# Layer 0 of a two-block transformer kernel: latent norms, up-projections and rotary rotation in one stage, with f32r products in 128-row chunks

## What is computed

```python
p = h @ w_in                                   # 384 cq | 256 ckv | 32 kr | 512 gq | 128 gk | 128 gv
qa = (rmsnorm(cq, q_norm) @ w_q_up)            # 8 heads of 64 + 32
kva = (rmsnorm(ckv, kv_norm) @ w_kv_up)        # 8 heads of 64 (keys) + 64 (values)
q_rope, k_rope = apply_rope(q_rope, ra), apply_rope(kr, ra)    # latent tokens only
qa = concat([q_nope, q_rope]) * (96 ** -0.5)
ka = concat([k_nope, broadcast(k_rope)])
qb, kb = apply_rope(rmsnorm(gq per head), rb) * (64 ** -0.5), apply_rope(rmsnorm(gk per head), rb)
```

## Time and profile before

| | |
|---|---|
| median of 3 runs | 3511.75 us (3507.56 to 3515.62) |
| profiled execution | 3518.39 us; its span 3516.5 us, mean granted TensorE clock 0.931 |
| PE busy | 3104.1 us, 88% of the span |
| DVE, ACT, POOL busy | 1457.6, 761.2, 237.0 us |
| ab_in, first to last PE instruction | 53.1 to 156.4 us |
| norm_qk, ab_up and rope together | 157.0 to 299.3 us |
| PE / DVE / ACT busy from 157.0 to 299.3 | 128.9 / 57.7 / 21.2 us |

### The profile page before, as it was taken

How to read it: one execution, slowest core, us unless ns; L and a number is a source line. 1 busy time by engine, 2 the same in 40 slices (tenths; PEclk the granted TensorE clock), 3 DMA queues, 4 the chain that set the end, 5 groups by cost and what they waited for, 6 DMA issues and landing times. The chain is left out here.

```text
span 3516.5 us, 48978 instructions
## 1 busy us (share of the span) xinstructions
PE 3104.1 (88%) x19193; PEld 2127.7 (61%) x19193; DVE 1457.6 (41%) x2568; ACT 761.2 (22%) x1482; POOL 237.0 (7%) x435
## 2 busy tenths in 40 slices
PE   7999998799886599977987759989999999899998
PEld 5734667333333598753333337867888788678886
DVE  4316564300000533852000026455555683655555
ACT  3114571211111302821111111142110111221101
POOL 0000040111111200001111110000000000000000
PEclk9999999899998699988998769999999999999998
DMA  7376812999998422349999973113334164123421
GB/s 259 123 269 153 207 18 95 384 419 419 419 419 349 132 72 61 74 164 388 419 419 418 419 283 115 60 49 90 95 107 109 39 104 61 49 72 95 125 72 54
DMA packets 352386, 675.09 MB, mean 192 GB/s; under 512 B 68643, under 2 KB 277636, under 8 KB 296775
## 3 DMA queue, kind: packets, MB, share of 16 engines
q1 hardware_dynamic: 336460, 635.42, 52.0%
q0 software_dynamic: 13664, 31.49, 2.5%
q10 hardware_dynamic: 2067, 5.48, 0.4%
HBM read 642.80 MB, written 45.09 MB: 196 GB/s over the span
## 5 line engine op out<-in xcount | busy, mean ns | idle before, releaser
L3838 ACT ACTIVATE ffn_mixed<-ffn_mixed 128x512 f32<-128x512 f32 x44 | 27.8, 632 | 393.8 <-DVE ffn_mixed L3759 393.8
L2054 DVE TENSOR_TENSOR moe0b_hidden<-moe0b_hidden,moe0b_wide_ps 64x512 f32<-64x512 f32 (+1 forms) x21 | 12.7, 602 | 229.1 <-ACT moe0b_hidden L2051 229.1
L2039 PE MATMUL moe0b_wide_ps<-moe_raw,moe0b_feats 128*64 128x512 f32 x208 | 95.7, 610 | 9.5 <-DMA moe_raw<-in_moe_w_up 9.5
L2054 DVE TENSOR_TENSOR moe1b_hidden<-moe1b_hidden,moe1b_wide_ps 64x512 f32<-64x512 f32 (+1 forms) x18 | 10.3, 573 | 224.1 <-ACT moe1b_hidden L2051 224.1
L2054 DVE TENSOR_TENSOR moe0b_second<-moe0b_second,moe0b_wide_ps 64x512 f32<-64x512 f32 (+1 forms) x20 | 12.2, 611 | 208.1 <-ACT moe0b_second L2051 208.1
L2054 DVE TENSOR_TENSOR moe1b_second<-moe1b_second,moe1b_wide_ps 64x512 f32<-64x512 f32 (+1 forms) x18 | 10.3, 572 | 211.4 <-ACT moe1b_second L2051 211.4
L2040 PE MATMUL moe0b_wide_ps<-moe_raw,moe0b_feats 128*64 128x512 f32 x208 | 95.9, 612 | 0.0
L3756 DVE TENSOR_SCALAR ffn_mixed<-ffn_gate_ps,all_cols 128x512 f32<-128x512 f32 x44 | 35.6, 810 | 145.3 <-PE ffn_up_ps L3688 141.1
L1496 DVE TENSOR_REDUCE attn_top<-attn_scores 128x1 f32<-128x768 f32 (+1 forms) x96 | 72.3, 776 | 37.1 <-PE attn_scores L1409 37.0
L1465 ACT ACTIVATE attn_probs_t<-attn_turned 128x512 f32<-128x512 f32 x112 | 63.4, 604 | 78.9 <-PE attn_turned L1423 78.9
L243 POOL CAST second_first_hi<-all_ahead 128x1024 fp32r<-128x1024 f32 x8 | 9.8, 1223 | 982.6 <-DMA all_ahead<-in_ffn_w_up 696.7
(11 more groups left out here) (998 smaller groups left out, 8681.3 us busy)
## 6 DMA issues: line engine op xcount, KB each, us to landing
moe_raw<-in_moe_w_gate SPq DMA_DIRECT2D x88, 1024.0 KB, 27.3
moe_raw<-in_moe_w_up SPq DMA_DIRECT2D x88, 1024.0 KB, 27.9
moe_raw<-in_moe_w_down SPq DMA_DIRECT2D x86, 1024.0 KB, 28.4
all_ahead<-in_ffn_w_up SPq DMA_DIRECT2D x88, 512.0 KB, 5.1
all_h<-in_moe_w_gate SPq DMA_DIRECT2D x26, 1024.0 KB, 26.8
all_h<-in_w_ada SPq DMA_DIRECT2D x23, 1024.0 KB, 5.5
all_h<-in_moe_w_down SPq DMA_DIRECT2D x21, 1024.0 KB, 28.3
ffn_down<-in_ffn_w_down SPq DMA_DIRECT2D x40, 512.0 KB, 3.6
```

The source lines that it names most:

```text
L2039: nc.tensor.matmul(wide_ps[n][LOW, :], x[:, c, :], gate[:, at], start=c == 0, stop=c == DC - 1)
L2054: return nc.vector.tensor_tensor(hidden[n][HIGH, 0:cols], hidden[n][HIGH, 0:cols], wide_ps[n][HIGH, 0:cols], ALU.mult)
L3838: nc.scalar.activation(mixed[s][:], mixed[s][:], ACT.Silu).then_inc(silu_ready, 1)
```

## The change

The three stages norm_qk, ab_up and rope become one, `up_stage`. In it:

- Queries and keys are computed in chunks of 128 rows instead of heads. The weights of the queries are loaded so that the rotary rows of four heads make a chunk (`q0`, `q1`) and the other rows of two heads make one (`q2` to `q5`). Two halves of 384 tokens take the place of 256 and 512. Every product is three f32r matmuls.
- The queries' products start from the raw latent times its gain; the root is applied to the result, when DVE takes it out of PSUM. The keys' and values' latent is scaled first.
- POOL gets work: the split of the query weights (beside ab_in), five of the ten squares, the rest part of the key and value weights, and the eight cosine products.
- The rotation has eight items: the shared key, the two rotary query chunks, four gq, gk.
- PSUM holds two slots of two banks, used in turn by 29 named uses (`UP_USES`); a use waits until the use before it in its slot has been taken.
- Units 16 to 23 of the conditioning move into ab_in, whose ring now has two slots (units 11 to 23); units 24 to 47 have a ring of three. ab_in starts with six DMAs of the query weights instead of units 11 and 12.
- The rotary tables are loaded over the query latent, so their five DMAs wait for `q5`.

```diff
-            own = [sb(f"ada_slot{n}", [PART, ada.GROUP])[:] for n in range(2)]
...
-            ada.place("in", own + [P.h[:].rearrange("p c n -> p (c n)")[:, n * ada.GROUP:(n + 1) * ada.GROUP] for n in range(3)], units)
-            early, late = units[0:2], units[2:]
+            units = range(FIRST_UNITS, 3 * DC)
+            ada.place("in", ada_slots[0:2], units)
+            coming_slots = [P.ahead[:].rearrange("p c n -> p (c n)")[:, n * ada.GROUP:(n + 1) * ada.GROUP] for n in range(2)]
+            ada.place("later", coming_slots + ada_slots[0:1], range(3 * DC, ada.GROUPS * DC))
...
-            at_unit = {8: early[0:1], 10: early[1:], 18: late[0:1], 19: late[1:2], 20: late[2:]}
+            at_unit = {11: (11,), 12: (12,), 13: (13,), 14: (14, 15), 15: (16,), 16: (17, 18), 17: (19,), 18: (20, 21), 19: (22,), 20: (23,)}
...
+        up_stage(nc, P, A, K, ada, weights, cq, ckv, lows, kr, gq, gk, qa, ka, va, distances)
```

The heart of `up_stage`, SP's tables and PE's products and first uses:

```diff
+            sp.wait_ge(ready, slots.made["q5"])
+            for q in range(QUADS):
+                sp.dma_start(rope_q[q * QUAD:(q + 1) * QUAD], K["rope_a"][rope_rows]).then_inc(tables_in, 16)
+            sp.dma_start(rope_g, K["rope_b"]).then_inc(tables_in, 16)
+            for u in range(33, 43):
+                ada.fetch(sp, u)
...
+            def q_rows(name, c, j):
+                cols = slice(j * PART, (j + 1) * PART)
+                for k, (w, x) in enumerate(((wq.hi, cq_hi), (wq.hi, cq_lo), (wq.lo, cq_hi))):
+                    for h in range(2):
+                        last = T.matmul(slot[slots.at[name]][:, h, 0:HALF], w[:, c, cols], x[:, c, h * HALF:(h + 1) * HALF],
+                                        start=c == 0 and k == 0, stop=c == QC - 1 and k == 2)
...
+            ada.multiply(pe, 24)
+            pe.wait_ge(cq_split, 1)
+            q_rows("q0", 0, 0)
...
+            spread("cq", NORM_CQ, 0)
+            q_product(1)
...
+            q_product(5)
+            ada.multiply(pe, 31)
...
+            k_product(0)
+            ada.multiply(pe, 32)
+            pe.wait_ge(tables_in, 16 * (2 + QUADS))
+            turn(0)
+            ada.multiply(pe, 33)
...
+            V.tensor_tensor(squares[0], cq[:, 0, :], cq[:, 0, :], ALU.mult).then_inc(squared_by["dve"], 1)
...
+            low_q(0)
...
+            emptied(dve, "cq")
+            take_rope(0)
```

More of the change, by code:

```diff
@@ L1235, in add_deep @@
     return take
-def load(slot, source, ring=0, after=None):
-    return Load(slot, source, ring, after)
-def product(operands, shape, take, load=0, engine=None, finish=None):
-    return Product(operands, shape, take, load, engine, finish)
 def wide(t):
@@ new lines, in v_product @@
+            def v_product(i):
+                enter(f"v{i}")
+                for n in range(2):
+                    rows = slice((2 * i + n) * PART, (2 * i + n + 1) * PART)
+                    for c in range(KVC):
+                        for k, (x, w) in enumerate(((ckv_hi, wkv_hi), (ckv_lo, wkv_hi), (ckv_hi, wkv_lo))):
+                            last = T.matmul(slot[slots.at[f"v{i}"]][:, n, :], x[:, c, rows], w[:, c, H_A * NOPE_A:],
+                                            start=c == 0 and k == 0, stop=c == KVC - 1 and k == 2)
+                last.then_inc(ready, 1)
@@ new lines, in spread, with turn @@
+            def spread(name, kind, group):
+                pe.wait_ge(inverted, group + 1)
+                enter(name)
+                quads.spread(slot[slots.at[name]], pick[:, kind], root[:, group, :], ready)
+            def turn(n):
+                x, rows = turn_rows[n]
+                enter(f"turn{n}")
+                T.matmul(slot[slots.at[f"turn{n}"]][rows, 0, :], swap[rows, rows], x, start=True, stop=True).then_inc(ready, 1)
+            ada.multiply(pe, 24)
+            pe.wait_ge(cq_split, 1)
@@ L1296, in _ @@
+            for h, (a, e) in enumerate(((0, BANK), (BANK, distances.SPAN))):
+                last = T.matmul(wide_rows("distance")[0:DSA_H, h, 0:e - a], distances.bias[:], distances.by_bucket[:, a:e], start=True, stop=True)
+            last.then_inc(ready, 1)
         @block.vector
         def _(dve):
[L1298 to L1308 removed]
+            V = nc.vector
@@ new lines, in share_key @@
+            def share_key(heads):
+                for h in heads:
+                    S.activation(ka[rope_rows, h, :], kr[rope_rows, :], ACT.Copy).then_inc(copied, 1)
+            round_q(0)
+            square(2, cq[:, 2, :])
+            round_q(1)
+            round_q(2)
+            square(3, ckv[:, 0, :])
+            take_root(0, FIRST)
+            act.wait_ge(ready, slots.made["cq"])
+            release(S.activation(halves(spread_q), full("cq"), ACT.Copy, scale=QK_A ** -0.5), "cq")
@@ new lines, in _ @@
+            share_key(range(6, H_A))
+            take_values(0)
+            ada.copy(act, 4)
+            take_values(1)
+            take_values(2)
+            ada.copy(act, 5)
+            act.wait_ge(ready, slots.made["distance"])
+            for h, (a, e) in enumerate(((0, BANK), (BANK, distances.SPAN))):
+                last = S.activation(distances.rows[:, a:e], wide_rows("distance")[0:DSA_H, h, 0:e - a], ACT.Copy)
+                last.then_inc(distances.made, 1)
+        @block.gpsimd
```

638 lines of the change are left out of this document (379 added, 259 removed), and 3 rows, old and new, of the table UP_USES.

## The result

| | before | changed |
|---|---|---|
| median of 4 runs each | 3511.11 us (3507.56 to 3515.62) | **3477.67 us** (3465.06 to 3482.88) |
| ratio, 95% interval | | 0.9899 (0.9868 to 0.9929) |
| span of the profiled execution | 3516.5 us | 3481.0 us |
| first matmul of ab_in to first of the attention | 246.3 us | 215.3 us |
| from there to the end | 3217.1 us | 3210.9 us |

The medians lie 33.4 us apart, the forecast was 35.4 (3476 us, range 3461 to 3495). The total came out. The profiled pair lies 35.5 us apart, and the table shows how: the stretch that the forecast was about gave only 31.0, the part behind it 6.2, and ab_in began 1.7 us later (54.8 for 53.1).

What follows compares the result with a forecast made beforehand. PE was taken to bound norm_qk, ab_up and rope (126.3 of 142.3 us). Products -29.6, rotation -6.2, ab_in's waits +3.6, the new stage's waits -3.2 sum to -35.4 us: 3511.75 to 3476 us, range 3461 to 3495.

Steps and rivals of the forecast that it cites:

- Products: Query, key and value products in the new stage: 35.4 us against 65.0, -29.6 us, at 0.174 per 384-column matmul.
- Units moved, 0, and ab_in's waits: Eight units and a transpose (8.6 us) move into ab_in, saving 0; units 15, 18, 21 wait, +3.6 us.
- Start: Start of the new stage: DVE's rest part waits for POOL's square by exclusion, PE waits 2.7 us; 0.9 without exclusion.
- Tables: Rotary tables land 7.8 us after `q5`; PE has 4.1 us of work and waits 3.7.
- Units: Late conditioning units in the new stage: unit 33 waits some 0.6 us behind the tables, unit 47 waits 0.4.
- Rival 2: Late units: landing at 8.0 us, ab_in's three waits grow 3.0 each, last units cost 3; -23 us, 3488, chance 0.12.
- Clock: PE at half clock for about 3 us after standing idle at the start; one fall charged at 1.7 us.
- What follows moves as a whole: Stages behind the new one, including the experts' weight fetches, start and end 35 us sooner.
- 1: Drains: PE waits for ten DVE operations delayed 1.5 us each by POOL, 15 us come back; -20, 3491, chance 0.14.
- 4: Slower: PSUM slots don't overlap, each of 29 uses waits for its 2.0 us drain; +21 us, 3532, chance 0.03.
- 3: Clock: two stretches of 8 us at half clock in the stage cost 8 instead of 1.7; -29, 3483, chance 0.10.
- 5: No gain: something else ends the stretch, or the experts' stream hides PE's saving; 3512, chance 0.05.

Runs made afterwards that it cites:

- the variant whose clock stayed at 1.00: The changed kernel with the last unit moved behind the last two rotations and its transposes behind the distances: stage 92.8 us, 3473.14 us.
- the variants that freed PE: Changed kernel with only the first f32r product of each chunk: stage 85.8 us, 3464.99 us; with three edits of order together: stage 92.1 us, 3468.22 us.
- the doubled drains: Changed kernel with DVE doing each operation that empties a PSUM slot into another tile twice, except in-place scalings: stage 102.1 us, 3488.97 us.
- the three comparisons: Unchanged sources of both kernels, changed against before, medians: 3477.67 against 3511.11 us, 3475.73 against 3510.61, 3475.06 against 3516.70.

## Why the prediction was right

The stage, term by term, with the mean of the three profiles of the changed kernel:

| us | forecast | measured |
|---|---|---|
| products | 35.4 | 38.3 |
| PE's other work | 46.5 | 45.1 |
| start (rest part of `cq`) | 2.7 | 1.1 (0.9, 1.2, 1.1) |
| slot of `q1` | 2.0 | 1.9 |
| tables | 3.7 | 1.7 (1.4, 2.2, 1.4) |
| units 33 to 47 | 1.0 | 4.3 (4.2, 2.9, 5.7) |
| last transpose | 0.8 | 0 |
| border to the attention | 0.9 | 1.1 |
| slow clock | 1.7 | 3.7 (4.4, 2.8, 3.8) |
| stage | 94.7 | 97.1 |

For the clock: PE was busy for 87.8, 86.2 and 87.3 us, and for 83.4 in the variant whose clock stayed at 1.00; the difference is the clock's. 83.4 less the products' 38.3 is the other work.

- **Products, the largest term, right in kind and 10% off in size.** The step "one of 384 columns ... I take the middle, 0.174" holds: 0.175. What was missed is 0.22 us for each of the 13 products, half where PE changes from f32 to f32r and half where it changes back. -26.7 us, not -29.6.
- **Rotation and the rest of PE's work**: a swap takes 0.95 to 1.05, for 1.03. The sums of squares were charged 0.48 each and take 0.35 to 0.39, which is most of the 1.4 us that this work came out under.
- **Units moved, 0, and ab_in's waits**: ab_in took 118.1, 117.5 and 114.9 us against 104.0, mean +12.8 for 12.2; its three waits sum to 3.0, 2.6 and 1.9 for 3.6. The cover held: POOL's split of the weights took 13.3 us, not the 8.8 worked out from the rows (below), and nobody waited.
- **Start: the exclusion is real, the step that used it failed.** "DVE's square to 0.95, POOL's to 2.8, the rest part to 3.75" lets POOL in between. POOL began at 1.41, behind the rest part's start at 1.03, and PE waited the 0.9 that the prediction gives for a start without exclusion. DVE was held up two operations later, where it cost PE 0.3 us at most.
- **Tables**: the step took 5.6 us for the last table from its issue, and 7.8 from `q5`. The last table landed 3.8, 4.7 and 3.9 us behind its issue, and from the end of `q5` (210.16) to PE going on (215.91) were 5.75.
- **Units: the term that was too small.** The prediction held two units late; four or five waits came, because behind the tables the DMA engines run at 1.01: around them, from 205 to 222 us, the medians from a unit's issue to its landing are 5.6 to 9.6 us, where 5.0 was taken. Rival 2 had 3 us for the last units; 3.3 came, from unit 33 on. Its other 9 us, in ab_in, did not: the three waits there sum to less than was forecast. Late units are also what bounded the variants that freed PE.
- **Clock**: one fall was charged at 1.7. In the three profiles there were three falls, two, and two of which one lasted twice as long, 3.7 us in the mean.

Measured against forecast, the stage's errors (+2.9 products, +3.3 units, +2.0 clock, +0.2 border; -2.0 tables, -1.6 start, -1.4 other work, -0.8 transposes, -0.1 slot) come to +2.5: the 97.1 for 94.7. The larger ones are as big as their sum; that they cancel is luck. The stretch gave 33.0 us of the 35.4 forecast. That the median met it to 2 us is luck too: the three comparisons gave 33.4, 34.9 and 41.6 us, and in the profiles 6.9 us came from behind the attention, about 5 of them from the wait at the experts' end. "What follows moves as a whole" was the step that failed there.

Of the rivals, 1 and 4 (drains) are refuted by the doubled drains; 3 (clock) is real, with stretches of 3.4 to 6.8 us and a cost of 3.7, not two of 8 us and a cost of 8; 5 is refuted by the time.

## What to carry to other kernels

Count f32 products by their columns: filling 128 rows gave 18.6 us here, more than twice what f32r with its two rest products gave (8.1). When PE's work shrinks around a fixed stream of loads, list every load of the ring again with the new distances, since the waits come back there, small and many; and cover a wait for a table with work that needs no table, because PE's stop can cost slow clock behind it as well. Before a difference in a stage is put down to an edit, take out what the clock did, by PE's busy time: here it made up 3.7 of 4.3 us. And profile the kernel before twice: a part that the change doesn't touch may differ too.

## What the runs showed of the hardware

- POOL can stand very long beside a DVE that issues without pause. In ab_in of the changed kernel a cast of the query weights took 4.08 us and the next ones 0.83:

```profile
64.01 4.08 POOL L1097 CAST l_wq_hi<-l_ka 128x768 fp32r<-128x768 f32 x1 [63.58 <-DMA l_ka<-in_mla_w_q_up]
...
66.19 1.22 DVE L933 CAST ab_in_w_hi<-all_ahead 128x2048 fp32r<-128x2048 f32 x1
67.44 2.79 DVE L935 TENSOR_TENSOR ab_in_last_low<-all_ahead,ab_in_w_hi 128x2048 fp32r<-128x2048 f32 x1
68.17 3.77 POOL L1099 TENSOR_TENSOR l_wq_lo<-l_ka,l_wq_hi 128x768 fp32r<-128x768 f32 x1
71.88 0.83 POOL L1097 CAST l_wq_hi<-l_ka 128x768 fp32r<-128x768 f32 x1
72.79 1.83 POOL L1099 TENSOR_TENSOR l_wq_lo<-l_ka,l_wq_hi 128x768 fp32r<-128x768 f32 x1
```

  DVE's operations from 63.78 to 66.19 each began some 0.08 us before the one ahead had ended; they kept their usual 0.95 and 0.42 us, and POOL stood. It got in where DVE left 0.03 us, between the end of its long cast (67.41) and 67.44: POOL's cast ended at 68.09, and DVE's operation took 2.79 us, where the same takes 2.29 elsewhere in ab_in. In all twelve profiles that operation takes 2.79 or 2.80 and POOL's cast ends some 0.65 us behind its start.
- Where PE changes from f32 to f32r matmuls the first pair takes 0.10 us more, and where it changes back the f32 one starts 0.09 late, with 0.25 us of idle time on its weight load that nothing explains; between two f32 products there is no such gap (4.07 us for a chunk of twelve).
- PE's clock fell to 0.50 behind stops of 0.9 to 2.9 us, for 3.4 to 10.2 us at a time, but not behind each: in the variant with the last unit later PE stopped for 1.9, 1.2, 1.5 and 1.8 us and the clock stayed at 1.00 to the end of the stage.
- A wait of 16.4 to 17.3 or of 22 us at the same instruction of the same stage, by which program it stands in, with nothing in the profile to explain it.
